# PEER late stage: one-hot tiles as bf16 with the token innermost, pair weight in three bf16 parts, all late low parts on GpSimd

## What is computed

```python
s = einsum('thpd,hpnd->thpn', q, sub_keys)        # two sets of 128 key scores per head
s_top, i_top = top_k(s, 16)
cand = s_top[:, :, 0, :, None] + s_top[:, :, 1, None, :]
best, pos = top_k(cand, 16)                       # 16 pairs (i, j) for each of 8 heads: 128 slots a token
g = softmax(best)
act = gelu(einsum('thkd,td->thk', u_tab[idx], xb))
out = einsum('thk,thkd->td', g * act, v_tab[idx]) # idx = i * 128 + j, 16384 experts
```

## Time and profile before

| | us |
|---|---|
| median of 3 runs | 2134.96 |
| the profiled execution, its own time | 2135.08 |
| its span | 2132.9 |
| PE busy | 2067.8 (97%) |
| DVE busy | 1501.6 (70%) |
| ACT busy | 1250.6 (59%) |
| POOL busy | 802.0 (38%) |

### The profile page before, as it was taken

The page is one execution under the profiler, slowest core; times in us unless marked ns, Lnnn a source line. Parts: engine busy times, 40 slices in busy tenths (PEclk is TensorE's granted clock), DMA queues, the critical chain, the costliest instruction groups (busy, mean ns, idle before and its releaser), DMA issues.

```text
span 2132.9 us, 40134 instructions
## 1 busy us (share of the span) xinstructions
PE 2067.8 (97%) x14238; PEld 1834.4 (86%) x14238; DVE 1501.6 (70%) x2698; ACT 1250.6 (59%) x2232; POOL 802.0 (38%) x569
## 2 busy tenths in 40 slices
PE   6999899999999999999998989999999999999998
PEld 3778899999999987777778879999999997777776
DVE  3436579736777778878778563996588887787785
ACT  3534444545666667767754634545566666676774
POOL 1010047754555522223302400688366652222330
PEclk9999999999999999999999989999999999999999
DMA  9745447775555678888864544456544447888883
GB/s 346 278 159 178 151 143 251 239 267 196 188 191 189 201 237 294 296 303 297 296 209 127 153 142 149 147 183 192 189 143 143 138 146 261 299 299 296 297 301 114
DMA packets 125494, 459.95 MB, mean 216 GB/s; under 512 B 14016, under 2 KB 14544, under 8 KB 124352
## 3 DMA queue, kind: packets, MB, share of 16 engines
q1 hardware_dynamic: 102976, 377.14, 52.9%
q0 software_dynamic: 21504, 79.53, 10.1%
q10 hardware_dynamic: 896, 1.76, 0.2%
HBM read 449.93 MB, written 8.44 MB: 215 GB/s over the span
## 4 chain that ended last, share of the span: by engine, by line
PE 92%; DVE 4%; DMA 2%; ACT 1%; issue 1%; SPq 0%; POOL 0%; DVEq 0%; ACTq 0%
PE pu L1332 12%; PE pu L1337 11%; PE pm L1408 11%; PE pm L1410 11%; PE pm L1409 11%; PE pu L1333 11%; PE pu L1202 4%; PE pu L1203 4%; PE pu L1204 4%; PE pm L1367 3%; PE pm L1366 2%; PE pm L1224 1%; PE pm L1672 1%; DMA arena<-in_ada 1%; DVE w_lo L1732 1%
## 5 line engine op out<-in xcount | busy, mean ns | idle before, releaser
L778 ACT ACTIVATE w_hi<-raw 128x1024 fp32r<-128x1024 f32 x600 | 634.0, 1057 | 445.7 <-PE pm L1410 225.4
L1732 DVE TENSOR_TENSOR w_lo<-raw,w_hi 128x1024 fp32r<-128x1024 f32 x444 | 572.3, 1289 | 388.2 <-ACT w_hi L778 377.3
L1332 PE MATMUL pu<-hid_split,w_hi 128*128 128x256 f32 x2048 | 500.3, 285 | 0.0
L1333 PE MATMUL pu<-hid_split,w_hi 128*128 128x256 f32 x2048 | 492.4, 280 | 0.0
L1408 PE MATMUL pm<-w_hi,hid_split 128*128 128x512 f32 x1024 | 405.0, 396 | 3.1 <-DVE hid_split L1995 3.1
L1332 PEld LDWEIGHTS pu<-hid_split,w_hi 128*128 128x128 f32 x2048 | 386.3, 189 | 24.5 <-issue 24.5
L1410 PE MATMUL pm<-w_lo,hid_split 128*128 128x512 f32 x1024 | 403.7, 394 | 0.0
L1409 PE MATMUL pm<-w_hi,hid_split 128*128 128x512 f32 x1024 | 402.9, 394 | 0.0
L1333 PEld LDWEIGHTS pu<-hid_split,w_hi 128*128 128x128 f32 x2048 | 386.1, 189 | 0.0
L577 POOL TENSOR_TENSOR w_lo<-raw,w_hi 128x1024 fp32r<-128x1024 f32 x96 | 229.9, 2396 | 188.4 <-ACT w_hi L778 188.4
L1337 PE MATMUL pu<-hid_split,w_lo 128*128 128x256 f32 x2048 | 290.5, 284 | 0.1
(11 more groups left out here) (276 smaller groups left out, 2931.5 us busy)
## 6 DMA issues: line engine op xcount, KB each, us to landing
raw<-in_u_tab SPq DMA_DIRECT2D x256, 512.0 KB, 3.6
raw<-in_v_tab SPq DMA_DIRECT2D x256, 512.0 KB, 3.5
raw<-in_ada SPq DMA_DIRECT2D x80, 512.0 KB, 3.7
raw<-in_wq SPq DMA_DIRECT2D x32, 512.0 KB, 3.5
raw<-in_gla_in SPq DMA_DIRECT2D x24, 512.0 KB, 4.7
raw<-in_rg_in SPq DMA_DIRECT2D x20, 512.0 KB, 3.5
arena<-in_ada SPq DMA_DIRECT2D x8, 1024.0 KB, 16.7
arena<-in_gla_state POOLq DMA_DIRECT2D x8, 512.0 KB, 14.0
```

What stands on the lines that cost most here:

```text
L778: act.activation(w_hi[:, s2, :], raw[:, s4, :], ACT.Copy).then_inc(hi_done, 1)
L1332: mm(pu[:, s, 0:SEQ], w_hi[:, s % 2, kk * P:kk * P + P], hid_hi[:, kk, 0:SEQ], start=(kk == 0), stop=False)
L1333: mm(pu[:, s, 0:SEQ], w_hi[:, s % 2, kk * P:kk * P + P], hid_lo[:, kk, 0:SEQ], start=False, stop=False)
L1732: tt_(w_lo[:, s2 if l2 is None else l2, :], raw[:, s4, :], w_hi[:, s2, :].bitcast(F32), ALU.subtract).then_inc(lo_done, 1)
```

## The change

It does the following.

1. The one-hot tiles `oh_b`, `oh_eq` and the products are bf16 and laid out [key, token] (token innermost, 4 tokens a key). The numbers 0 to 127 are held as a bf16 tile `iota_t` of the same layout.
2. The routing splits each weight into three bf16 parts whose sum is the float32 weight, with seven DVE instructions for each prompt group, and turns i, j and the two smaller parts as bf16 (`sel_p`) and the largest as float32 (5 transposes instead of 3).
3. A late step makes three products: ACT multiplies by the largest part, into part 0 of `oh_w`; DVE by the two others (`times_rest`); POOL by none. PE makes 3 matmuls a token instead of 2: 12 a step, bf16.
4. POOL forms the low part of every late tile, in one instruction of 1024; DVE forms none there.
5. ACT applies gelu before it rounds the next tile, where it was after.

```diff
-POOL_ALL = POOL_LOWS + LATE // 2
+POOL_ALL = POOL_LOWS + LATE
...
-        oh_b = sb("oh_b", [P, TOKS, NKEY], F32R)
-        oh_hi = sb("oh_hi", [P, TOKS, NKEY], F32R)
-        oh_eq = sb("oh_eq", [P, TOKS, NKEY], BF16)
-        sel_w = sb("sel_w", [P, 2, T], F32R)
+        oh_b = sb("oh_b", [P, NKEY, TOKS], BF16)
+        oh_w = sb("oh_w", [P, 3, NKEY, TOKS], BF16)
+        iota_t = sb("iota_t", [P, NKEY, TOKS], BF16)
+        ident_b = sb("ident_b", [P, P], BF16)
+        oh_eq = sb("oh_eq", [P, NKEY, TOKS], BF16)
+        sel_w = sb("sel_w", [P, SEQ])
...
-                def low_part(i, c, slot, part):
-                    half = slice(part * (D // 2), part * (D // 2) + D // 2)
+                def late_low(i, c, slot):
                     pool.wait_ge(hi_done, i * 4 + (m0 + EARLY + c + 1))
...
+                    pool.tensor_tensor(w_lo[:, c % 2, :], raw[:, slot, :], w_hi[:, c % 2, :].bitcast(F32),
+                                       ALU.subtract).then_inc(lo_pool, 1)
...
                     for t in range(TOKS):
-                        last = act.activation(oh_hi[:, t, :], oh_eq[:, t, :], ACT.Copy,
-                                              scale=sel_w[:, 0, bass.ds(i * 16 + (c * TOKS + t), 1)].bitcast(F32))
+                        last = act.activation(oh_w[:, 0, :, t], oh_eq[:, :, t], ACT.Copy,
+                                              scale=sel_w[:, bass.ds(i * 16 + (c * TOKS + t), 1)])
...
                     act.wait_ge(split_used, i * 4 + (m0 + EARLY + c + 1))
+                    gelu_in_place(c)
                     if lay == 0:
...
-                    gelu_in_place(c)
...
-                    for a, at in enumerate((pm[:, 1, 0:SEQ], pm[:, 1, SEQ:2 * SEQ], pm[:, 0, 0:SEQ])):
-                        last = pe.transpose(at[:, tt * P:tt * P + P], slot[:, a, :], ident)
+                    if lay == 0:
+                        pe.wait_ge(iota_set, 2)
+                    for a in range(4):
+                        pe.transpose(sel_p[:, a, tt * P:tt * P + P], part_b[:, a, :], ident_b[:])
+                    last = pe.transpose(pm[:, 0, tt * P:tt * P + P], part_f[:, 0, :], ident)
...
                     for t in range(TOKS):
                         out = pm[:, 2 + s % 2, t * P:t * P + P]
-                        mm(out, oh_b[:, t, :], oh_hi[:, t, :], start=True, stop=False)
-                        last = mm(out.rearrange("p (a n) -> p a n", a=4), oh_b[:, t, :], oh_lo[:, t], start=False, stop=True)
+                        for part in range(3):
+                            last = mm(out, oh_b[:, :, t], oh_w[:, part, :, t], start=(part == 0), stop=(part == 2))
                     last.then_inc(oh_used, 1)
...
+                    pe.wait_ge(lo_pool, i * 4 + (lay * POOL_ALL + POOL_LOWS + s + 1))
                     u_low(s % 4, s % 2)
...
+                    dve.tensor_copy(part_b[:, 0:2, :], slot[:, 0:2, :])
+                    link(dve.tensor_copy(part_b[:, 2, :], slot[:, 2, :]))
+                    link(dve.tensor_copy(part_f[:, 0, :], part_b[:, 2, :]))
+                    link(tt_(part_f[:, 1, :], slot[:, 2, :], part_f[:, 0, :], ALU.subtract))
+                    link(dve.tensor_copy(part_b[:, 2, :], part_f[:, 1, :]))
+                    link(dve.tensor_copy(part_f[:, 2, :], part_b[:, 2, :]))
+                    tt_(part_b[:, 3, :], part_f[:, 1, :], part_f[:, 2, :], ALU.subtract).then_inc(slot_ready, 1)
...
-                link(dve.tensor_copy(sel_w[:, 0, 0:SEQ], pm[:, 0, 0:SEQ]))
-                tt_(sel_w[:, 1, 0:SEQ], pm[:, 0, 0:SEQ], sel_w[:, 0, 0:SEQ].bitcast(F32), ALU.subtract).then_inc(sel_ready, 1)
...
+                dve.tensor_copy(sel_w[:], pm[:, 0, 0:SEQ]).then_inc(sel_ready, 1)
+
+                def selected(i, c, part):
+
+                    return sel_p[:, part, bass.ds(i * 16 + c * TOKS, TOKS)].unsqueeze(1).to_broadcast([P, NKEY, TOKS])
...
+                    tt_(oh_eq[:], iota_t[:], selected(i, c, 0), ALU.is_equal).then_inc(eq_ready, 1)
...
+                    tt_(oh_b[:], iota_t[:], selected(i, c, 1), ALU.is_equal).then_inc(ob_ready, 1)
+
+                def times_rest(i, c):
+
+                    dve.wait_ge(eq_ready, i * 4 + (g0 + c + 1))
+                    for part in (1, 2):
+                        last = tt_(oh_w[:, part], oh_eq[:], selected(i, c, part + 1), ALU.mult)
+                    last.then_inc(oh_lo_ready, 1)
...
                     if final < 2:
                         second_hot(i, c + 1)
-                    if c % 2 == 0:
-                        low(i * 4 + (m0 + EARLY + c + 1), slot, 1)
+                        times_rest(i, c + 1)
```

More of the change, by code:

```diff
@@ L320, in build_step @@
         eps_set = sem("eps_set")
+        iota_set = sem("iota_set")
         hid_full = sem("hid_full")
@@ L412, in u_freed @@
                 eng.wait_ge(lo_done, LOWS[f"uv{lay}"] + c - POOL_LOWS + 1)
-            elif c % 2 == 0:
-                eng.wait_ge(lo_pool, lay * POOL_ALL + POOL_LOWS + late)
             else:
-                eng.wait_ge(lo_done, LOWS[f"uv{lay}"] + EARLY - POOL_LOWS + late)
+                eng.wait_ge(lo_pool, lay * POOL_ALL + POOL_LOWS + c - EARLY + 1)
         def v_freed(eng, lay, c):
@@ L630, in peer_pool @@
                 if lay == 0:
-                    for c in range(0, LATE, 2):
-                        late_two(0, c, u_load(0, EARLY + c + 2)[0] if c + 2 < LATE else 0, c + 2 == LATE)
-                else:
[L634 to L638, removed]
+                    for c in range(LATE):
+                        late_low(0, c, u_load(0, EARLY + c)[0])
+                else:
+                    with pool.Fori(0, LATE // 4) as i:
+                        for c in range(4):
+                            late_low(i, c, c)
@@ L1971, in product, with u_late @@
                     tt_(one, one, pu[:, s % 4, 0:SEQ].unsqueeze(1), ALU.mult).then_inc(u_prod, 1)
-                def u_late(i, c, slot, first=False, final=0):
+                def u_late(i, c, first=False, final=0):
                     if final < 2:
                         second_hot(i, c + 1)
-                    if c % 2 == 0:
-                        low(i * 4 + (m0 + EARLY + c + 1), slot, 1)
+                        times_rest(i, c + 1)
                     dve.wait_ge(oh_used, i * 4 + (g0 + c + 1))
@@ L2029, in peer @@
                     for c in range(LATE - 1):
[L2030 removed]
+                        u_late(0, c, first=(c == 0), final=c // (LATE - 2))
                 else:
                     for c in range(4):
[L2033 removed]
+                        u_late(0, c, first=(c == 0))
                     with dve.Fori(1, LATE // 4 - 1) as i:
                         for c in range(4):
[L2036 removed]
+                            u_late(i, c)
                     for c in range(3):
[L2038 removed]
+                        u_late(LATE // 4 - 1, c, final=c // 2)
                 low(m0 + NKEY, 0, 0)
```

35 lines of the change are left out of this document (11 added, 24 removed).

## The result

The changed kernel takes 2202.00 us (median of 4 runs, 2201.50 to 2204.61) against 2134.68 (median of 4 runs, 2133.82 to 2136.32): a ratio of 1.0317, with a 95% interval of 1.0299 to 1.0335. It is 67 us slower where the prediction said 14 faster, and it lies outside the range of 2109 to 2156. It lies 9 us above the 2193 of the first rival.

A forecast was written before the change was run, and what follows sets the result against it. TensorE (PE) alone was taken to set the pace in the late steps. A 15.0 us gain on one-hot products less 0.9 for transposes gave -14.1, from 2134.96 to 2121 us; the range was 2109 to 2156.

The forecast's parts named there:

- the first rival: Late one-hot products on PE: weight load stays the pace or moving operand read at half rate, 0.111 each; 2193 us, chance 0.18.
- The step that failed: PE's 12 strided one-hot operands a late step, 8 bytes between elements: no row to price them, stride costed at nothing.
- the upper end: Highest pace allowed for a bf16 one-hot product: weights loaded as slowly as now, 0.111 us, a loss of 56.8 us.
- x: Pace of one bf16 one-hot product on PE in a late step, taken as 0.060 us, bounded by 0.053 and 0.111.
- The sign named for a wrong forecast: One-hot weight loads standing 0.08 us or more apart, or PE waiting at the one-hot block for `oh_lo_ready`.
- The formula: PE's gain per late step, 0.777 - 11x us: forecast 0.117 a step, 15.0 us over 128 steps.
- the second rival: Late one-hot products on PE: load cheaper but not quite hidden, pace 0.085 us; 2156 us, chance 0.12.
- The estimate by the 81 ns: Skill's sustained rate for load and matmul pairs of 128 columns, applied to late steps: loss of 14.6 us, 2150 us.
- The transposes: Routing's turns on PE going from 3 to 5 at 4 places, 8 more at 0.11 us: cost 0.9 us.
- the doubled rate: DVE's late-step bf16 work at two elements a cycle: 2.3 us a step against 3.56 at full price, hidden either way.
- Routing: Seven small DVE instructions per group, about 1.8 us, up to 4.3, within 7.4 us of slack: costed at nothing.
- The third rival: DVE's bf16 work stays at full price and a helper sets late steps of 3.65 to 3.75 us; 2127 to 2139, chance 0.10.

The follow-up runs named there:

- e2_moving_runs: Changed kernel, but PE reads only the moving operand `oh_w` as 128 adjacent elements, weights still 8 bytes apart (wrong product); 2113.91 us.
- k1_pairs: Changed kernel, complete, one-hot tiles holding two tokens side by side instead of four, so PE reads at 4 bytes; 2116.48 us, ratio 0.9911 to the kernel before.
- e1_both_runs: Changed kernel, but PE reads both one-hot operands as 128 adjacent elements instead of every fourth (wrong product); 2115.02 us.
- k2_runs: Changed kernel, complete, only `oh_w` stored key innermost, so PE reads it adjacent and DVE and ACT read `oh_eq` at 8 bytes; 2115.95 us, ratio 0.9906.
- e8_low_split: `k1_pairs` with the low parts of odd late tiles back on DVE, POOL forming the even ones; 2116.98 us, ratio 0.9914 to the kernel before.

## Why the prediction was wrong, point by point

**The step that failed** is one sentence, a term of the sum that was put at nothing: "I cost the stride at nothing, and a stride that halves the read rate is within the upper end (0.107 to 0.111)". The stride cost the whole loss and the gain besides: `e2_moving_runs` differs from the change only in how PE reads the moving operand, and takes 88 us less. The upper end was passed by a little (0.1175 against 0.111, since a halved rate is 2 x 0.058, and the end had been taken from the weight load), and it was kept as a bound, not as a case: two causes that could slow x were put into one rival at 0.18, and the range left it out. The matmuls of the earlier trace rows and the transposes of the earlier trace rows all read adjacent elements, so nothing there said anything on an operand with a step. A cost without any row, in each of 1536 products, deserved a case and a chance of its own, and a range that reaches to its end. The sign named for a wrong forecast came: the loads stand about 0.11 apart, and PE does not wait for `oh_lo_ready`. One sum of the prediction is off as well, though nothing hangs on it: x = 0.066 gives 2129, not the 2127 that ends its own range.

**The formula** held: 0.777 - 11x is -0.52 us a step at the measured pace against the 0.53 seen, and 0.777 - 11 x 0.058 = 0.139 against the 0.13 of `k1_pairs`. It missed one small thing: the first bf16 load starts 0.23 us after the last `u_high` load, not 0.117, and the float32r load behind the block follows sooner instead (in `k1_pairs` 0.89 us lie between the last `u_high` load and the first `u_low` load, before it was 1.02).

**x for adjacent elements** was forecast at 0.060 and measured at 0.0565 (`e1_both_runs`, (0.84 - 0.219) / 11) to 0.058. The expectation that the bf16 weight load hides was right, and the second rival with its 0.085 did not come. The estimate by the 81 ns for a stream of load and matmul pairs, in the Trainium skill, "TensorE: Matmul & The Clock Gate", section "Back-to-back issue gap", was not met either: the pairs here went at 56 to 58 ns, and with a strided operand at 117.

**The first rival** gave 2193 and named two mechanisms in one breath. The second of them, the halved read, is the one that the runs bear out: the pace doubles with the step of the moving operand alone; the 9 us that the result lies above it are the pace of 0.1175 in place of 0.111 (11 x 0.0065 x 128 = 9.2). The first, a weight load one column at a time, was refuted by the same runs; the row cited for it, that the pace followed the weight columns, is true of float32r and said nothing of bf16.

**The transposes** were priced at 0.9 us. At 0.06 the four bf16 turns and the one that stayed float32 take 4 x 0.06 + 0.11 = 0.35 us against 3 x 0.11 before: 0.02 more at each of 4 places, so the term is about zero.

**DVE** went at the doubled rate, 0.42 us as forecast for that case, although one source lies in PSUM; only the table in the Trainium skill, "VectorE: DVE Perf Modes", section "The perf-mode tier table", spoke against it. `k2_runs` shows that the types alone are not enough: with `oh_eq` read across the tile and the part repeated along the innermost run, it falls back to 0.68. Which of the two does it was not tried. As forecast, it did not change the sum.

**ACT** took 1.51 us for the four products, 0.23 more than before, within the cover of 1.6 us.

**POOL** took 2.40 us for each low part, as forecast, and PE waited for none of them; `e8_low_split` shows that the move is worth nothing.

**Routing** stayed hidden, but by less than I thought. The seven new instructions were forecast at 1.8 us, and up to 4.3 with two of them held beside POOL's low part. At the tightest place, layer 1's first group, they took 6.1 us (the timelines of DVE and of PE after):

```profile
1422.82 0.29 DVE L1897 CAST arena<-arena 128x256 bf16<-128x256 f32 x1
...
1423.28 2.31 DVE L1899 CAST arena<-arena 128x128 f32<-128x128 bf16 x1
...
1425.95 2.40 DVE L1901 CAST arena<-arena 128x128 bf16<-128x128 f32 x1
...
1428.64 0.29 DVE L1903 TENSOR_TENSOR arena<-arena 128x128 bf16<-128x128 f32 x1
```

```profile
1430.16 0.40 PE L1304 MATMUL pm<-ident_b,arena 128*128 128x128 bf16 x4
```

Two casts with one source took 2.3 and 2.4 us each. POOL's low parts ran from 1423.06 to 1425.51 and from 1425.87 to 1428.26, and each cast ended 0.1 us after one of them. I had counted only the two subtractions as held, at the 1.56 of the earlier trace rows; they took 0.29 in each of the four groups, and the casts were held instead. The group is ready at 1428.93 and turned at 1430.16: of 7.4 us of slack 1.2 are left. In another group (404.80 to 412.99) the seven took 8.2 us, 0.8 more than the slack here; that group was turned only at 417.42.

**The third rival** did not come: the bf16 work kept the doubled rate, and even `k2_runs`, with DVE's two products at full price, stands at 2115.95. A DVE with the full 3.56 us a step was not run.

The forecast of 2121 thus fits the kernel in which PE's operand is not 8 bytes apart: `k1_pairs` takes 2116.5, and the 5 us between are the smaller x (128 x 11 x 0.002 = 2.8), the transposes (0.9) and about 1 us that I did not trace, within the spread of the runs.

## What to carry to other kernels

Where PE is the bound, look first at the byte step of the operand that moves through it: here, for bf16, 4 bytes were nearly free, 8 bytes doubled the time of a product. A layout that makes one engine faster is paid for by the one that reads the tile, so price both, and give a cost that no row shows a full case of its own. Two neighbours of 2 bytes were enough to serve both DVE's doubled rate and PE, and where DVE has idle time, storing the tile for PE alone was just as good.

## What the runs showed of the hardware that was not expected

- The time of a bf16 product follows the step of its moving operand above 4 bytes: 0.058, 0.063, 0.1175 and 0.23 us at 2, 4, 8 and 16 bytes. The weights' step of 8 bytes cost 15 ns of load (98 to 113) and, behind 128 adjacent columns, no time that could be seen (2113.91 us against 2115.02); behind columns 8 bytes apart it cost 0.003 us of pace.
- A load of 128 bf16 weight columns takes 98 ns in the records, of float32r 192, and the pair of load and matmul goes at 0.0565 against 0.111. 0.0565 is 0.44 ns a column, near the 0.46 of a float32r product of 256 columns (0.117), so my reading is that with bf16 the columns are the bound, with float32r the load.
- DVE's `tensor_tensor` on bf16 took 0.42 us for 512 elements with one source in PSUM and a broadcast in the middle of its shape, as long as two tokens lay side by side; with one source read across the tile 0.68.
- A cast on DVE of 128 elements in SBUF took 2.3 to 2.4 us when it began while POOL's low part ran or with it, ending 0.1 us after it, against 0.21 to 0.23 when it began before that or clear of it. Which pairs of operands are held was not tried.
- ACT slows with the step of the tile that it writes. By source line, the products of 128 elements took 387 ns to a dense tile, 430 with 4 bytes between elements of both source and target and 567 with 8; with 8 in the source and a dense target they took 398:

```profile
L908 ACT ACTIVATE oh_hi<-oh_eq,sel_w x512: 384/387/407, 490.0 to 1755.8; 128x128 fp32r<-128x128 bf16 x171
```

```profile
L883 ACT ACTIVATE oh_w<-oh_eq,sel_w x512: 418/430/466, 491.1 to 1737.9; 128x128 bf16<-128x128 bf16 x171
```

```profile
L883 ACT ACTIVATE oh_w<-oh_eq,sel_w x512: 552/567/605, 490.9 to 1823.3; 128x128 bf16<-128x128 bf16 x171
```

```profile
L883 ACT ACTIVATE oh_w<-oh_eq,sel_w x512: 388/398/436, 491.2 to 1738.5; 128x128 bf16<-128x128 bf16 x171
```

The first is the kernel before (it writes float32r, so the comparison with it is loose), the second `k1_pairs`, the third the change, the fourth `k2_runs`.
